# A decoder of HGRN, dilated attention, GLA and NSA layers: pieces of a dense unit between the level scores, other orders around GLA, one rounding moved ahead of a logarithm

## What is computed

```
forget = lb + (1 - lb) * sigmoid(f);  key = 1 - forget;  query = silu(q);  log_f = log(forget)
b = cumsum(log_f)                                   # in a chunk
scores[t, s] = sum_k q[t,k] * k[s,k] * exp(b[t,k] - b[s,k])   for s <= t
o = scores @ v + (q * exp(b)) @ state
state = exp(b_last) * state + (k * exp(b_last - b))^T @ v
out = rmsnorm(o, gain) * silu(g)
swiglu: (silu(u @ w_gate) * (u @ w_up)) @ w_down
```

## Time and profile before

| | us |
|---|---|
| three runs | 2410.38, 2420.55, 2421.78 (median 2420.55) |
| the profiled execution's own time | 2419.04 |
| its span, first to last instruction | 2416.9 |
| TensorE busy | 2278.3 (94%) |
| VectorE busy | 924.5 (38%) |
| ScalarE busy | 878.0 (36%) |
| GpSimd busy | 1142.8 (47%) |
| mean granted clock of TensorE | 0.957 |

### The profile page before, as it was taken

The page is one execution under the profiler, slowest core; times in us unless marked ns, Lnnn a source line. Parts: engine busy times, 40 slices in busy tenths (PEclk is TensorE's granted clock), DMA queues, the critical chain, the costliest instruction groups (busy, mean ns, idle before and its releaser), DMA issues.

```text
span 2416.9 us, 28100 instructions
## 1 busy us (share of the span) xinstructions
PE 2278.3 (94%) x10190; PEld 1846.5 (76%) x10190; DVE 924.5 (38%) x1557; ACT 878.0 (36%) x1257; POOL 1142.8 (47%) x621
## 2 busy tenths in 40 slices
PE   5899989999998999999999996999899999999998
PEld 3688877888886988887888884878755667888886
DVE  4354445332333047734323414242475004331332
ACT  4455554432323224334422224423354224331322
POOL 3766745554554455445545542624100335553552
PEclk9989999999999999999999998988899999999999
DMA  3211112332332322123322331212100223232331
GB/s 126 62 47 58 61 34 89 96 107 85 97 107 66 96 79 79 44 92 98 98 101 95 99 101 70 83 44 70 62 0 25 89 88 96 87 112 80 98 108 71
DMA packets 53250, 193.25 MB, mean 80 GB/s; under 512 B 6816, under 2 KB 7728, under 8 KB 52912
## 3 DMA queue, kind: packets, MB, share of 16 engines
q1 hardware_dynamic: 50688, 184.95, 24.1%
q10 hardware_dynamic: 2480, 7.19, 0.8%
HBM read 187.92 MB, written 4.19 MB: 79 GB/s over the span
## 4 chain that ended last, share of the span: by engine, by line
PE 84%; DVE 6%; issue 3%; ACT 3%; POOL 3%; DMA 0%; SPq 0%; DVEq 0%; POOLq 0%; ACTq 0%
PE ps L358 21%; PE ps L359 21%; PE ps L360 21%; PE ps L445 3%; PE ps L866 2%; PE ps L810 2%; PE ps L833 2%; PE ps L518 1%; PE ps L519 1%; PE ps L520 1%; POOL w_split L1301 1%; PE ps L820 1%; DVE arena L1488 1%; PE ps L575 1%; PE ps L577 1%
## 5 line engine op out<-in xcount | busy, mean ns | idle before, releaser
L1301 POOL TENSOR_TENSOR w_split<-ring,w_split 128x1024 fp32r<-128x1024 f32 (+2 forms) x319 | 816.8, 2561 | 1090.6 <-ACT w_split L884 1090.6
L358 PE MATMUL ps<-u_split,w_split 128*128 128x512 f32 x1768 | 714.1, 404 | 39.4 <-POOL u_split L1310 18.1
L884 ACT CAST w_split<-ring 128x1024 fp32r<-128x1024 f32 (+2 forms) x319 | 347.5, 1089 | 1019.0 <-PE ps L360 914.4
L359 PE MATMUL ps<-u_split,w_split 128*128 128x512 f32 x1768 | 701.1, 397 | 0.0
L360 PE MATMUL ps<-u_split,w_split 128*128 128x512 f32 x1768 | 700.5, 396 | 0.0
L358 PEld LDWEIGHTS ps<-u_split,w_split 128*128 128x128 f32 x1768 | 340.9, 193 | 125.4 <-issue 33.1
L359 PEld LDWEIGHTS ps<-u_split,w_split 128*128 128x128 f32 x1768 | 340.8, 193 | 72.2 <-issue 2.9
L360 PEld LDWEIGHTS ps<-u_split,w_split 128*128 128x128 f32 x1768 | 339.6, 192 | 73.6
L358 PE MATMUL ps<-hid,w_split 128*128 128x512 f32 x656 | 256.1, 390 | 1.6 <-POOL hid L1393 1.6
L360 PE MATMUL ps<-hid,w_split 128*128 128x512 f32 x656 | 255.2, 389 | 0.0
L359 PE MATMUL ps<-hid,w_split 128*128 128x512 f32 x656 | 255.2, 389 | 0.0
(11 more groups left out here) (236 smaller groups left out, 2497.5 us busy)
## 6 DMA issues: line engine op xcount, KB each, us to landing
ring<-in_w_hgrn SPq DMA_DIRECT2D x32, 512.0 KB, 3.6
ring<-in_w_attn_qk SPq DMA_DIRECT2D x24, 512.0 KB, 3.6
ring<-in_w_merge SPq DMA_DIRECT2D x24, 512.0 KB, 3.4
ring<-in_w_gu0a SPq DMA_DIRECT2D x22, 512.0 KB, 3.6
ring<-in_w_gu0b SPq DMA_DIRECT2D x22, 512.0 KB, 3.6
ring<-in_w_gu1a SPq DMA_DIRECT2D x22, 512.0 KB, 3.6
ring<-in_w_gu1b SPq DMA_DIRECT2D x22, 512.0 KB, 3.5
ring<-in_w_gu2a SPq DMA_DIRECT2D x22, 512.0 KB, 3.5
```

The source lines that it names most:

```text
L358: nc.tensor.matmul(ps[:, bank], ws[:, 0, r, w], act[:, 0, c], start=c == 0, stop=False)
L359: nc.tensor.matmul(ps[:, bank], ws[:, 0, r, w], act[:, 1, c], start=False, stop=False)
L884: nc.scalar.copy(ws[:, 0, slot, 0:w], ring[:, r, 0:w]).then_inc(s["w_hi"], 1)
L1301: nc.gpsimd.tensor_tensor(ws[:, 1, slot, 0:w], ring[:, r, 0:w], ws[:, 0, slot, 0:w].bitcast(F32), ALU.subtract).then_inc(s["w_lo"], 1)
```

## The change

The change moves work; it adds none to TensorE and leaves every product as it was.

1. `unit` takes a `part` (lo, hi) of its eight column tiles. In an HGRN head, unit 2 of the next head is cut in `THIRDS` and laid behind the first three level groups, and unit 3 in halves before and behind the chunk states. In GLA each head's level groups are laced likewise with one `mid` unit: kv0, r1, q1, r2. The units between the other steps of GLA move up accordingly.
2. VectorE, HGRN: silu of the output gate and the next head's gates come ahead of the first level copy, the scan behind level 5, the level exponents behind levels 4, 3, 1 and 0.
3. ScalarE, HGRN: the sigmoid of the next head's output gate moves from behind the head's rounding of its output to behind the copy of the value, ahead of the output's square.
4. ScalarE, feed-forward: `early_norm` rounds the third unit ahead of `rms`; the first two tiles are written out ahead of the loop.
5. GLA: the section `mid` has q1 before wv0; `nsa_rotate` uses banks 4 and 5 for the queries; VectorE splits a rotation into `times_sin` and `add_sin` and does the eight block inputs of both sets before the first head's gating; ScalarE and GpSimd round the second `nsa_tm` unit before the first decay factors.

```diff
-MID = ["kv0", "kv1", "r0", "k0", "r1", "k1", "q0", "wk0", "wk1", "wv0", "wv1", "q1", "q2", "q3", "r2", "r3"]
+MID = ["kv0", "kv1", "r0", "k0", "r1", "k1", "q0", "wk0", "wk1", "q1", "wv0", "wv1", "q2", "q3", "r2", "r3"]
...
-                pe.wait_ge(s["w_lo"], v)
-                for c in range(n):
+                lo, hi = part or (0, n)
+                if lo == 0:
+                    pe.wait_ge(s["w_lo"], v)
+                for c in range(lo, hi):
...
+            THIRDS = ((0, 3), (3, 6), (6, 8))
...
                     m.then_inc(s["score_ps"], 1)
+                    if n < len(LEVEL_PAIRS):
+                        between(n - 1)
...
-                chunk_scores(head, head, dec, key[x], qry[x], ALL)
+                more = head != HEADS_H - 1
+                chunk_scores(head, head, dec, key[x], qry[x], ALL,
+                             between=lambda n: hgrn_project(nxt, 2, part=THIRDS[n]) if more else None)
...
-                if head != HEADS_H - 1:
-                    hgrn_project(nxt, 2)
+                if more:
+                    hgrn_project(nxt, 3, part=(0, 4))
                 pe.wait_ge(s["kt_ready"], cnt(head, 1, 1))
                 chunk_states(lambda c: kT[:, c], lambda c: vT[:, c])
-                if head != HEADS_H - 1:
-                    hgrn_project(nxt, 3)
+                if more:
+                    hgrn_project(nxt, 3, part=(4, 8))
...
                 hi(nxt, 1)
+                hi(nxt, 2)
                 rms(n)
...
                     hgrn_value(nxt)
+                    hgrn_sigmoid(nxt, 2, sg_, "sig_g")
                     hi(*hgrn_unit(nxt2, 1)) if not isinstance(head, int) else hi("hgrn_out", 1)
                 output_square(head, osq)
...
-                if more:
-                    hgrn_sigmoid(nxt, 2, sg_, "sig_g")
                 if not isinstance(head, int):
                     hi(*hgrn_unit(nxt2, 3))
...
-            gla_scores(0)
+            gla_scores(0, "kv0")
             gla_keys(0)
-            mid("kv0")
+            mid("kv1")
             gla_states(0)
-            mid("kv1")
+            mid("r0")
             gla_outputs(0)
-            mid("r0")
+            mid("k0")
             output_mean_square(HEADS_H, gosq)
-            mid("k0")
-            gla_scores(1)
-            mid("r1")
+            gla_scores(1, "r1")
             gla_states(1)
...
             compress_hidden(0)
-            gla_scores(2)
+            gla_scores(2, "q1")
             gla_keys(1)
             compress_hidden(1)
             gla_states(2)
-            mid("q1")
+            mid("q2")
             gla_outputs(2)
-            mid("q2")
+            mid("q3")
             output_mean_square(HEADS_H + 2, gosq)
-            mid("q3")
             compress_out()
-            gla_scores(3)
+            gla_scores(3, "r2")
+            gla_states(3)
             compressed_scores()
-            gla_states(3)
-            mid("r2")
             gla_outputs(3)
-            mid("r3")
-            output_mean_square(HEADS_H + 3, gosq)
             nsa_rotate(2)
             nsa_rotate(3)
-
+            output_mean_square(HEADS_H + 3, gosq)
+            mid("r3")
```

More of the change, by code:

```diff
@@ L57 @@
     _n += _units
-MID = ["kv0", "kv1", "r0", "k0", "r1", "k1", "q0", "wk0", "wk1", "wv0", "wv1", "q1", "q2", "q3", "r2", "r3"]
+MID = ["kv0", "kv1", "r0", "k0", "r1", "k1", "q0", "wk0", "wk1", "q1", "wv0", "wv1", "q2", "q3", "r2", "r3"]
 MID_UNIT = {name: k for k, name in enumerate(MID)}
 MID_BANK = {name: n % 2 for n, name in enumerate(m for m in MID if m[0] != "w")}
-PLAIN = [("mid", k) for k in range(7, 11)] + [("merge", 3 * j + 2) for j in range(DC)]
+PLAIN = [("mid", k) for k, name in enumerate(MID) if name[0] == "w"] + [("merge", 3 * j + 2) for j in range(DC)]
 SPLIT = [(name, k) for name, units, _ in SECTIONS for k in range(units) if (name, k) not in PLAIN]
@@ L348, in plain, with unit @@
                 return m
-            def unit(section, k, act, bank, i=None, per=0, n=8, ready=None):
+            def unit(section, k, act, bank, i=None, per=0, n=8, ready=None, part=None):
                 r, v, _ = split_use(section, k, i, per)
-                pe.wait_ge(s["w_lo"], v)
-                for c in range(n):
+                lo, hi = part or (0, n)
+                if lo == 0:
+                    pe.wait_ge(s["w_lo"], v)
+                for c in range(lo, hi):
                     if ready is not None:
@@ L421, in _, with hgrn_project, chunk_scores @@
             FREED = ("sig_f", "query", "silu_g", "vf_ready")
-            def hgrn_project(head, k, ready=None):
+            def hgrn_project(head, k, ready=None, part=None):
                 name, first, *loop = hgrn_unit(head, k)
-                if head != 0:
+                if head != 0 and (part is None or part[0] == 0):
                     pe.wait_ge(s[FREED[k]], cnt(later(head, -1), 1, 1))
-                used(unit(name, first, us, BANK[k], *loop, ready=ready))
-            def chunk_scores(head, it, dv, k_, q_, rows, first_x=True):
+                m = unit(name, first, us, BANK[k], *loop, ready=ready, part=part)
+                if part is None or part[1] == 8:
+                    used(m)
+            def chunk_scores(head, it, dv, k_, q_, rows, first_x=True, between=lambda n: None):
                 for c in range(NCH):
@@ L664, in _, with mid @@
                          "q2": ("nt_ready", 10), "q3": ("nt_ready", 11), "r2": ("nt_ready", 12), "r3": ("nt_ready", 13)}
-            def mid(name):
-                sem, v = MID_FREED[name]
-                pe.wait_ge(s[sem], v)
-                used(unit("mid", MID_UNIT[name], us, MID_BANK[name]))
+            def mid(name, part=None):
+                if part is None or part[0] == 0:
+                    sem, v = MID_FREED[name]
+                    pe.wait_ge(s[sem], v)
+                m = unit("mid", MID_UNIT[name], us, MID_BANK[name], part=part)
+                if part is None or part[1] == 8:
+                    used(m)
             ROT_AFTER = (8, 9, 10, 11, 12, 13)
-            ROT_BANK = (2, 3, 0, 1, 0, 1)
+            ROT_BANK = (2, 3, 4, 5, 4, 5)
             def nsa_rotate(x):
@@ L688, in compress_hidden @@
                 for half in range(2):
[L689 removed]
+                    r, v = ring_use("mid", MID_UNIT[("wk", "wv")[x] + str(half)])
                     pe.wait_ge(w_ready[r], v)
@@ L721, in gla_scores @@
                 pe.wait_ge(s["gv_ready"], TT)
-                chunk_scores(I, HEADS_H + p, gdec, kg[:, p], qg[:, p], rows, first_x=hh % 2 == 0)
+                chunk_scores(I, HEADS_H + p, gdec, kg[:, p], qg[:, p], rows, first_x=hh % 2 == 0,
+                             between=lambda n: mid(weave, THIRDS[n]))
             def gla_keys(p):
@@ L938, in tile @@
                         last = j == HC - 1
-                        hi(down, 0) if last else hi(gu, 2 * j + 2, i, 4)
+                        if last:
+                            hi(down, 0)
+                        elif half or j:
+                            hi(gu, 2 * j + 2, i, 4)
                         act.wait_ge(s["gate_norm"], at(G + j + 1, 2))
@@ L945, in tile @@
                         nc.scalar.copy(dst, gtmp[:, x]).then_inc(s["g_hi"], 1)
-                    with act.Fori(0, (HC - 1) // 2) as i:
-                        tile(0, i)
-                        tile(1, i)
+                    tile(0)
+                    tile(1)
+                    with act.Fori(0, (HC - 3) // 2) as i:
+                        tile(2, i)
+                        tile(3, i)
                     tile(HC - 1)
@@ L1447, in _ @@
             ahead("gla_lr", 0)
-            for n in range(3):
+            for n in range(4):
                 ahead("gla_v", n)
@@ L1689, in prepare @@
                 def prepare(n):
-                    if n == 2:
+                    if n == 0:
+                        dve.wait_ge(s["scores"], cnt(head, 8, 1))
                         hgrn_silu(head)
```

82 lines of the change are left out of this document (42 added, 40 removed).

## The result

Measured beside each other, four runs each: the kernel before took 2417.1 us (median, 2410.4 to 2421.8), the changed one 2390.0 us (2375.8 to 2395.8). The ratio is 0.9881, 95% interval 0.9846 to 0.9917, so 27 us less. Six more runs of the changed kernel on another occasion gave 2389.7 us. The profiled execution is the slowest of its four: 2395.8 us, its span 2394.0. Against the profile before (span 2416.9) that is 22.9 us less; the forecast was 41.

A forecast was written before the change was run, and what follows sets the result against it. The prediction took a chain through VectorE, ScalarE and POOL, as long as the head, to bound HGRN, and low clock and waits to cost GLA. Its terms, 9 + 6.4 + 4.5 + 21 = 41 us, took 2419.0 to 2378; range 2360 to 2403.

The forecast's parts named there:

- What bounds HGRN: HGRN heads: the chain through VectorE, ScalarE and POOL is as long as the head, 37.5 us; the change makes it 36.1.
- rival 3: HGRN's dense units: laced waits for POOL make them start at 1.2 GHz, 2 us per head; 2390 us; chance 0.13.
- Rival 2: HGRN breaks free of the chain through POOL, to some 34 us per head; 23 us instead of 9, 2364; chance 0.10.
- HGRN's 9 us: HGRN heads 0 to 6: 1.0 us less for head 0, 1.5 each for heads 1 to 5, 0.8 for head 6.
- Slack 2.8 us: cost nothing: ScalarE in HGRN: the moved sigmoid's table loads, 2.6 us per head, are covered before TensorE needs the output's square.
- Feed-forward starts: Three feed-forward starts: TensorE's 2.12 us wait for POOL goes at each, 6.4 us in all; bounds 0 and 7.
- Token-major unit: Second token-major unit before GLA: rounding and low half ahead of the first decay factors gain 4.5 us; bounds 0 and 6.4.
- GLA's 21 us: GLA, four heads of laced level scores: 28.6 us gained less 7.4 owed, 21 us; bounds 8 and 34.
- rival 4: Level groups stay slow although laced, in GLA too; only waits are gained, 16 us, and HGRN 0; 2403 us; chance 0.13.
- The second token-major unit's low half: POOL before GLA: the low half is held until VectorE's exponents are done and comes at 1553.5.
- The rule that stands beside the sum in the prediction: GpSimd shares SBUF interfaces with VectorE when VectorE has two SBUF inputs; without it the sum is 1.9 larger.
- The slower rival: ScalarE becomes the bound in HGRN: late squares cost seven heads 32 us in all; 2440 us; chance 0.04.

The follow-up runs named there:

- e_chain_again: Rerun of e_chain, the changed kernel with ScalarE rounding the first unit of the head after next ahead of its exponential of the last three levels; 2365.4 us.
- e_ffn: The kernel before with the feed-forward part of the change alone; ratio 0.9957 to the kernel before.
- e_gla: The kernel before with the third mixer's part alone: token-major unit ahead of the decay factors, laced GLA levels, other order there; ratio 0.9921 to the kernel before.
- e_again: The changed kernel itself, measured again beside three of the repairs; 2389.7 us, ratio 0.988 to the kernel before.
- e_tail: The changed kernel with POOL's cosines ahead of merge's second unit's low half and VectorE's sine products ahead of the additions, in the third mixer's end; 2381.2 us.
- e_hgrn: The kernel before with the HGRN part alone: laced units 2 and 3, VectorE's new order, sigmoid ahead of the output's square; ratio 0.999 to the kernel before.
- e_head7: The changed kernel with, in head 6 alone, the gate's sigmoid back behind the rounding of the head's output; 2373.6 us, ratio 0.9834 to the kernel before.
- e_lace: The kernel before with the HGRN lacing on TensorE alone, VectorE's and ScalarE's orders as before; 2457.9 us, ratio 1.0167 to the kernel before.
- e_order: The kernel before with HGRN's new orders on VectorE and ScalarE but no lacing on TensorE; 2433.4 us, ratio 1.0063 to the kernel before.
- e_diag: The changed kernel with VectorE building the value part's block inputs behind the second GLA head's diagonal instead of ahead; 2390.0 us, ratio 0.9886 to the kernel before.
- e_best: The changed kernel with all four repairs together: head 6's sigmoid, ScalarE's rounding, the third mixer's end, the block inputs; 2366.5 us, ratio 0.9778 to the kernel before.

## Why the prediction was right, and where it was not

The time, 2390, lies inside 2360 to 2403, and faster by over 0.5% was the likeliest case. The size was too large: 27 of 41 us. Part by part, each alone, the sum had 6.4, 9 and 25.5 us (feed-forward, HGRN, third mixer) and the runs gave 10.4, 2.4 and 19.1. So HGRN and the third mixer were both sized too large. The feed-forward part made up for some of it by luck: its 10.4 us lie above its term and above the 7.1 that its profile shows, for no reason that is known.

*What bounds HGRN: right.* The chain through VectorE, ScalarE and POOL is shown by four kernels with 20.0 to 20.2 us behind the last exponent and by e_chain_again, where that piece is 17.9 us. The period was forecast at 36.1, and 36.3 came out. The waits, the gates' 0.3 us and the full clock in laced stretches (rival 3's opposite) stand in the profile. Rival 2 didn't happen in the change; e_chain shows what it would have taken.

*HGRN's 9 us: wrong, 0.0 in the profile and 2.4 alone.* Two terms failed. The first is the gain in heads 0 to 5, 8.5 us by the forecast. It took 18.2 us to the end of the last exponent before and 16.8 after. In heads at a full clock they are 17.9 (e_ffn) and 17.2, so 0.74 us a head, 4.4 in all, and not 1.4; part of the 37.5 us that it started from was a low clock in that one execution, which other executions of the same code don't have. The second is "Slack 2.8 us: cost nothing" of the moved sigmoid. It took the 5.4 us between outputs and square from a head that has a unit of the head after next there. Head 6 has none. Its cover was gone, and the price was 3.2 us, near the 2.6 that the text set for that case. The sum allowed head 6 a gain of 0.8, and 31.22 to 30.43 is just that, but by chance: the undisturbed head 6 of before takes 28.2 (e_ffn, e_gla). Head 7, of which the forecast said nothing, is no effect of the change. It takes some 15 or 22.4 us in either code; the one profile of before had the short form, the one of after the long.

*Feed-forward starts: right.* 2.35 us each where 2.12 was the term, since the matmuls behind the wait run faster too. *Token-major unit: right*, 5.4 us for 4.5, the wait now 1.05.

*GLA's 21 us: right in its mechanism, 14.1 and 18.7 us in two profiles of the same kernel.* The forecast wanted near 150 us at a clock of 0.93 or more from the first diagonals to the first NSA scores; it is 164.2 us at 0.90, and 159.5 in e_again. By head, before and in e_again: 38.8 to 36.0, 44.0 to 39.4, 45.8 to 34.9, 49.7 to 49.3. The laced levels of heads 0, 2 and 3 run at full clock in e_again (1.00; 0.65, 0.57 and 0.73 before), so rival 4 fell there. Those of head 1 don't: 0.81 over their 17.9 us in both profiles, dense pieces among them. The wait for the diagonal that was to stay at 2.1 is 1.75. The 4.5 us charged for the sparse stretch were not paid. Against that the clock still falls behind head 1's diagonal (0.75 over 13.6 us), which wasn't in the sum, and the tail's wait was 5.50 for a forecast 4; with its repair in e_tail the last head takes 45.4 us.

*The second token-major unit's low half: right.* The forecast had it held up on POOL until VectorE's exponents were done, and landing at 1553.5, from the earlier trace rows. It ends at 1553.89, after 5.93 us; the same operation took 2.54 us in the kernel before. The rule that stands beside the sum in the prediction agrees with that too.

```profile
1547.96 5.93 POOL L1312 TENSOR_TENSOR w_split<-ring,w_split 128x1120 fp32r<-128x1120 f32 x1 [2.84 <-ACT w_split L891]
```

VectorE's exponents and a scan run beside it until 1551.50, and the 2.4 us from there to its end are about what it takes alone. No run takes them away, so the cause isn't isolated.

*The slower rival* had its place right (ScalarE's sigmoid ahead of the square) and its reach wrong: it holds in one head of seven. Two of the signs that the forecast named against itself did show, each in one place: TensorE waits 2.45 us for ScalarE's square behind head 6, and the clock is low between laced pieces in GLA's head 1.

## What to carry to other kernels

When work is laced into a phase that feeds another engine, that engine gets its inputs later; measure the lacing and the new order of the consumer apart, since here each alone made the kernel slower by 37 and 13 us and together they were worth 2.4. Find the chain that closes a loop's period and move what isn't part of it out of its way: one rounding on an engine that sat idle for 3.4 us was worth 12.8 us, more than the whole HGRN part. When a cover is named for a moved step, look at the last iterations, which lack it. And read a loop's period from more than one execution before a gain is taken off it: 0.6 of the 37.6 us here were a low clock that came and went with the execution.

## What was not expected of the hardware

- The clock of a stretch can have two outcomes for the same code. Head 7 took 14.2 to 15.2 us in six profiles (before, e_hgrn, e_head7, e_chain_again, e_lace, e_order) and 22.4 in seven (after, e_again, e_tail, e_diag, e_best, e_ffn, e_gla), there at a granted clock of 0.51, in kernels with long and with short waits before it (2.46 and 5.08 us ahead of e_order's short form, 0.69 and 3.65 ahead of e_best's long one). In the six the granted clock is full again 1.9 to 3.4 us behind the head's start, in the seven not before 20.9 us. What decides it stays open. The Trainium skill (TensorE: Matmul & The Clock Gate, What's actually happening) says that the window in which the chip judges TensorE's activity runs free of the kernel, so that the point of a change of clock differs from run to run; that would fit two outcomes for one code, and no run here isolates it.
- GLA's second head is alike: 36.3 us (e_chain_again) or 39.4 (after, e_again, e_tail, e_diag, e_best) behind the same wait of 1.75 us.
- POOL's low half of a 1120-column unit took 5.93 us when it began beside VectorE's exponents and scan (after) and 2.54 us with VectorE idle (before).
- One execution ran for 5477 us with a mean matmul of 802 ns, where 400 is usual, while the granted clock in its record stood at 1.00.
